# A Mamba-2 scan's chunk loop: `mix` on VectorE, one GpSimd wait fewer, and the w_out split taken two pieces at a time

## What is computed

```python
# token mixing: attention and a bidirectional Mamba-2 scan side by side, one output projection
attn = mla_attention(q_nope, q_rope, k_nope, krope_all, v)          # 4 heads, 128 queries at a time
y = y_f + flip(y_b) + d_skip[:, None] * xs                          # the scan, chunks of 128 tokens
y = y.reshape(b, l, SSM_WIDTH) * silu(z)
ssm_out = rms_norm(y, g_out)                                        # y * rsqrt(mean(y*y)+eps) * g_out
out = concatenate([attn, ssm_out], axis=-1) @ w_out

# inside the scan, for each chunk c of 128 tokens, 8 heads of 64, state 128
lmat  = exp(where(causal, a_cs[..., :, None] - a_cs[..., None, :], -inf))
y_diag = einsum("bgcls,bgrcls,bcsgrp->bclgrp", cb, lmat, xr)        # cb: scores of C against B
state  = state * chunk_decay + chunk_states
y_off  = einsum("bclgn,cbgrpn,bgrcl->bclgrp", cc, entering, exp(a_cs))
```

## Time and profile before

| | |
|---|---|
| median of three runs | 1767.8 us (1766.47 to 1768.09) |
| the profiled execution: time, span | 1768.09 us, 1766.3 us |
| TensorE busy | 1677.5 us, 95% of the span |
| VectorE, ScalarE, GpSimd busy | 1040.2, 725.2, 74.6 us |
| mean granted TensorE clock | 0.982 |
| chunk loop of the scan | about 392 to 480 us |
| attention; its last head | 481 to 801 us; from 738 us |

### The profile page before, as it was taken

One profiled execution on the slowest core, in us unless ns is written; L12 is line 12 of the kernel. 1 busy time (PEld: TensorE's weight loads), 2 busy tenths in 40 slices (PEclk: granted clock), 3 DMA queues, 4 the chain that ended last, 5 costly groups with the idle time before them and its releaser, 6 DMA issues. The chain is left out here.

```text
span 1766.3 us, 24765 instructions
## 1 busy us (share of the span) xinstructions
PE 1677.5 (95%) x9795; PEld 1500.1 (85%) x9795; DVE 1040.2 (59%) x1581; ACT 725.2 (41%) x1208; POOL 74.6 (4%) x116
## 2 busy tenths in 40 slices
PE   6999899999799999999997999999999998999997
PEld 6787788878678888887887999999999997888885
DVE  5855765328755555574568554555545554467777
ACT  5652323334544444463564333333333333434453
POOL 0100000004300000000000000000000000000000
PEclk9999999999999999999999999999999999999998
DMA  9134242002400000114321222222222225573345
GB/s 370 70 131 139 108 147 75 25 33 54 119 14 19 1 13 1 66 37 156 124 96 37 100 86 84 91 88 93 95 82 85 101 76 194 187 234 97 121 145 196
DMA packets 76290, 176.33 MB, mean 100 GB/s; under 512 B 10352, under 2 KB 26944, under 8 KB 74128
## 3 DMA queue, kind: packets, MB, share of 16 engines
q1 hardware_dynamic: 72080, 169.75, 27.7%
q0 software_dynamic: 4096, 5.01, 0.9%
HBM read 131.02 MB, written 43.70 MB: 99 GB/s over the span
## 5 line engine op out<-in xcount | busy, mean ns | idle before, releaser
L409 PE MATMUL psF<-gv,gu_ring 128*128 128x320 f32 x1232 | 382.5, 310 | 9.2 <-issue 4.6
L410 PE MATMUL psF<-gv,gu_ring 128*128 128x320 f32 x1232 | 382.0, 310 | 0.0
L411 PE MATMUL psF<-gv,gu_ring 128*128 128x320 f32 x1232 | 382.0, 310 | 0.0
L409 PEld LDWEIGHTS psF<-gv,gu_ring 128*128 128x128 f32 x1232 | 232.5, 189 | 10.1 <-issue 9.1
L410 PEld LDWEIGHTS psF<-gv,gu_ring 128*128 128x128 f32 x1232 | 232.4, 189 | 0.0
L411 PEld LDWEIGHTS psF<-gv,gu_ring 128*128 128x128 f32 x1232 | 232.3, 189 | 0.0
L409 PE MATMUL psF<-d_w_ring,d_hid_ring 128*128 128x512 f32 x360 | 141.4, 393 | 6.3 <-DVE d_w_ring L2687 6.3
L410 PE MATMUL psF<-d_w_ring,d_hid_ring 128*128 128x512 f32 x360 | 141.6, 393 | 0.0
L411 PE MATMUL psF<-d_w_ring,d_hid_ring 128*128 128x512 f32 x360 | 141.4, 393 | 0.0
L409 PE MATMUL psP<-hT_hi,win_hi 128*128 128x512 f32 (+1 forms) x336 | 122.9, 366 | 2.3 <-DVE hT_lo L184 1.6
L411 PE MATMUL psP<-hT_hi,win_lo 128*128 128x512 f32 (+1 forms) x336 | 119.7, 356 | 0.0
(11 more groups left out here) (425 smaller groups left out, 3622.2 us busy)
## 6 DMA issues: line engine op xcount, KB each, us to landing
hid_variants<-hraw SPq DMA_DIRECT2D x77, 320.0 KB, 2.2
d_hid<-hid_variants SPq DMA_DIRECT2D x77, 320.0 KB, 3.0
m_wring<-in_w_mod SPq DMA_DIRECT2D x16, 1024.0 KB, 5.5
d_b<-in_w_down SPq DMA_DIRECT2D x44, 256.0 KB, 3.8
win_raw<-in_w_in SPq DMA_DIRECT2D x18, 512.0 KB, 5.7
w_mod_staged<-in_w_mod SPq DMA_DIRECT2D x16, 512.0 KB, 11.8
raw_gu<-in_w_gate SPq DMA_DIRECT2D x11, 512.0 KB, 3.9
raw_gu<-in_w_up SPq DMA_DIRECT2D x11, 512.0 KB, 4.8
```

What stands on the lines that cost most here:

```text
L409: pe.matmul(out, w_hi, x_hi, start=first, stop=False, skip_group_check=onto)
L410: pe.matmul(out, w_hi, x_lo, start=False, stop=False, skip_group_check=onto)
L411: return pe.matmul(out, w_lo, x_hi, start=False, stop=last, skip_group_check=onto)
```

## The change

It has four parts.

1. In the scan, the copy of the turned y (`mix`) moves from ScalarE to VectorE, where it is also multiplied with `g_out`. It is done two chunks late, ahead of the off reads; the last two stand after the loop.
2. w_out is accordingly split without the gain, with a plain copy and a plain subtraction.
3. The semaphores `off_f_read` and `off_b_read` become one, `off_read`, raised after both reads. The contribution of chunk 9 moves into the loop, ahead of the diagonal products, and `next_state` is written in line, for every chunk. GpSimd's `decay` no longer waits for `y_ready`.
4. In the last head of attention, the pieces of w_out are split in pairs at t = 2, 4 and 6, on ScalarE after the exponents and on VectorE after the maximum.

```diff
GpSimd, decay(c)
                 pool.wait_ge(sf_ready, c + 1)
-                if c >= 1:
-                    pool.wait_ge(y_ready, c)
                 pool.tensor_tensor(heads(decayed[:]), heads(sf[:, c % 2, :]), across(cdrow[:, c, 0:8], SP_), ALU.mult
...
             # ScalarE: mix(c), its calls mix(c - 1) in the loop and mix(NT - 1) behind it are gone
-            def mix(c):
-                act.wait_ge(y_turned, c + 1)
-                act.activation(zt(c), quads(A[0]), ACT.Copy).then_inc(mix_ready, 1)
...
             # VectorE
+            def mix(c):
+                dve.wait_ge(y_turned, c + 1)
+                dve.tensor_tensor(zt(c), A[0].rearrange("p (a t) -> p a t", a=4),
+                                  across(L.cols[:, C_GS:C_GS + 4], P), ALU.mult).then_inc(mix_ready, 1)
...
             for c in range(NT):
+                if c >= 2:
+                    mix(c - 2)
                 dve.wait_ge(off_done, c + 1)
                 if c >= 2:
                     dve.wait_ge(yn_ready, c - 1)
-                dve.tensor_tensor(heads(yv...), heads(A[1]), ..., ALU.mult).then_inc(off_f_read, 1)
-                dve.tensor_tensor(heads(off_b[:]), heads(A[2]), ..., ALU.mult).then_inc(off_b_read, 1)
-                dve.wait_ge(off_f_read, c + 1)
-                dve.wait_ge(off_b_read, c + 1)
+                f.mark(dve.tensor_tensor(heads(yv...), heads(A[1]), ..., ALU.mult))
+                f.link(dve.tensor_tensor(heads(off_b[:]), heads(A[2]), ..., ALU.mult))
+                dve.sem_inc(off_read, 1)
                 f.link(dve.tensor_tensor(yv[:, c % 2, :], yv[:, c % 2, :], off_b[:], ALU.add))
-                if c + 1 < NT:
-                    next_state(c)
+                (the body of next_state(c))
+                if c + 1 < NT:
                     weights_in_chunk(c + 1)
                 dve.wait_ge(diag_done, c + 1)
...
-            next_state(NT - 1)
+            mix(NT - 2)
             for d in range(2):
                 dve.wait_ge(fin_mm, d + 1)
                 dve.tensor_copy(st_in[:, d, :, :], ...).then_inc(fin_cp, 1)
+            mix(NT - 1)
...
             # TensorE
                 if c >= 1:
-                    pe.wait_ge(off_b_read, c)
+                    pe.wait_ge(off_read, c)
...
                 if c + 1 < NT:
                     segments(c + 1)
-                    pe.wait_ge(off_f_read, c + 1)
-                    contribution(NS + c, c, 0, A[1])
+                pe.wait_ge(off_read, c + 1)
+                contribution(NS + c, c, 0, A[1])
+                if c + 1 < NT:
                     scores(c + 1)
...
-            pe.wait_ge(off_f_read, NT)
-            contribution(NS + NT - 1, NT - 1, 0, A[1])
...
     # OutProj
-        gain = self.L.cols[:, C_GS + k - 4:C_GS + k - 3] if k >= 4 else 1.0
-        act.activation(self.part(k, 0), self.raw(k), ACT.Copy, scale=gain).then_inc(self.hi, 1)
+        act.activation(self.part(k, 0), self.raw(k), ACT.Copy).then_inc(self.hi, 1)
...
     # attention, ScalarE; before: one wo.act_hi(act, t - 2) at each t, ahead of exp at even t and behind it at odd t
+                        if h == HEADS - 1 and t in (2, 4, 6):
+                            act.wait_ge(proj, n_proj(HEADS))
+                            for n in (t - 2, t - 1):
+                                wo.act_hi(act, n)
                         if t >= 4:
                             out(u // 2 - 2)
...
     # attention, VectorE; before: one at each t, at odd t between the pt_lo of groups 0 and 1
+                    if h == HEADS - 1 and t in (2, 4, 6):
+                        for n in (t - 2, t - 1):
+                            wo.dve_lo(dve, n)
                     if t % 2 == 0 and t >= 4:
                         out(u // 2 - 2)
```

More of the change, by code:

```diff
@@ L515, in phase_front @@
         (ones_set, xwf_ready, st_loaded, st_turned, sch, z_done, z_copied, x_turned, x_copied, xw_ready, s_mm,
-         s_ready, cb_done, cb_read, seg_done, exp_done, off_done, off_f_read, off_b_read, w_ready, diag_done, y_ready, squared,
+         s_ready, cb_done, cb_read, seg_done, exp_done, off_done, off_read, w_ready, diag_done, y_ready, squared,
          rstd_ready, yn_ready, y_turned, mix_ready, sf_ready, dec_ready, fin_mm, fin_cp, consts, pch) = (
@@ L520, in phase_front @@
                  "x_copied", "xw_ready", "s_mm", "s_ready", "cb_done", "cb_read", "seg_done", "exp_done", "off_done",
-                 "off_f_read", "off_b_read", "w_ready", "diag_done", "y_ready", "squared", "rstd", "yn_ready", "y_turned", "mix_ready",
+                 "off_read", "w_ready", "diag_done", "y_ready", "squared", "rstd", "yn_ready", "y_turned", "mix_ready",
                  "sf_ready", "dec_ready", "fin_mm", "fin_cp", "consts", "pch"))
@@ L930, in _ @@
                     scale(c - 1)
-                    mix(c - 1)
             square(NT - 1)
             scale(NT - 1)
-            mix(NT - 1)
         @block.vector
@@ L1168, in weights_in_chunk @@
                 dve.tensor_tensor(w, w, cb[:].unsqueeze(2).to_broadcast([P, 2, 4, P]), ALU.mult).then_inc(w_ready, 1)
-            def next_state(c):
+            weights_in_chunk(0)
+            for c in range(NT):
+                if c >= 2:
+                    mix(c - 2)
+                dve.wait_ge(off_done, c + 1)
+                if c >= 2:
+                    dve.wait_ge(yn_ready, c - 1)
+                f.mark(dve.tensor_tensor(heads(yv[:, c % 2, :]), heads(A[1]), across(eoff[:, c, 0:8], SP_), ALU.mult))
+                f.link(dve.tensor_tensor(heads(off_b[:]), heads(A[2]), across(eoff[:, c, 8:16], SP_), ALU.mult))
+                dve.sem_inc(off_read, 1)
+                f.link(dve.tensor_tensor(yv[:, c % 2, :], yv[:, c % 2, :], off_b[:], ALU.add))
                 dve.wait_ge(s_mm, NS + c + 1)
@@ L1521, in act_hi @@
             act.wait_ge(self.extra_loaded, 32)
-        gain = self.L.cols[:, C_GS + k - 4:C_GS + k - 3] if k >= 4 else 1.0
-        act.activation(self.part(k, 0), self.raw(k), ACT.Copy, scale=gain).then_inc(self.hi, 1)
+        act.activation(self.part(k, 0), self.raw(k), ACT.Copy).then_inc(self.hi, 1)
     def dve_lo(self, dve, n):
         k = self.ORDER[n]
-        hi = self.part(k, 0).bitcast(F32)
         dve.wait_ge(self.hi, n + 1)
[L1529 to L1534, removed]
+        dve.tensor_tensor(self.part(k, 1), self.raw(k), self.part(k, 0).bitcast(F32), ALU.subtract).then_inc(self.lo, 1)
     def first_mixes(self):
@@ L1715, in _ @@
                         pt(u - 3, 2)
-                    ahead = h == HEADS - 1 and 2 <= t < 2 + wo.AHEAD
                     if t % 2 == 1:
@@ L1722, in _ @@
                         exp(u - 1)
-                        if ahead:
-                            wo.act_hi(act, t - 2)
                         if t == 1 and h % 2 == 1:
@@ L1727, in _ @@
                     else:
-                        if ahead:
-                            act.wait_ge(proj, n_proj(HEADS))
-                            wo.act_hi(act, t - 2)
                         if t >= 2:
@@ L1850, in _ @@
                         split(h + 1)
-                    ahead = h == HEADS - 1 and 2 <= t < 2 + wo.AHEAD
-                    if ahead and t % 2 == 0:
-                        wo.dve_lo(dve, t - 2)
+                    if h == HEADS - 1 and t in (2, 4, 6):
+                        for n in (t - 2, t - 1):
+                            wo.dve_lo(dve, n)
                     if t % 2 == 0 and t >= 4:
@@ L1856, in _ @@
                     if t >= 2:
[L1857 to L1861, removed]
+                        pt(u - 2, 0, 2)
                     if t >= 1:
```

10 lines of the change are left out of this document (removed).

## The result

The changed kernel took 1775.59 us (median of seven) beside 1767.01 us for the kernel before: a ratio of 1.0054, interval 1.0038 to 1.007. In a second set it took 1777.1 us beside 1764.18 us, a ratio of 1.0093 (1.0077 to 1.0109). A ratio is given here with its 95% interval and is not the quotient of the two medians. It is slower: by 8.6 and 12.9 us in the medians, by 9.5 and 16.4 us if the ratios are taken. 1779.3 was forecast, 11.5 us slower, from 1773 to 1784.

What follows compares the result with a forecast made beforehand. The prediction took TensorE to bound the scan's chunk loop. Its terms, 1.0 + 3.75 + 0 + 0.8 + 4.1 + 1.9 = 11.55 us, on the median of 1767.8 gave 1779.3 us, range 1773 to 1784.

Steps and rivals of the forecast that it cites:

- TensorE bounds the loop, and VectorE's margin is spent: Scan's chunk loop: TensorE sets the 7.95 us period; VectorE's off reads end 0.95 and 0.35 us before the next contribution.
- `decayed` beside the weights: 0.75 us a chunk: Scan's chunk loop: without its wait, `decayed` blocks VectorE's weight lines about 0.9 to 0.95 us; period 8.7 for 7.95.
- By chunk: C(n) is the start of chunk n's contribution on TensorE: C(1) +1.0, C(2) to C(6) +3.75, C(7) +0, C(8) +0.8 us.
- The tail: +4.1: End of the scan: `mix` of chunk 8 comes 4.1 us later, and all of it passes into attention.
- The last head: +1.9: Attention's last head, w_out pieces in pairs: +2.1 us at t=2, -0.1 each at t=4 and t=6.
- The sum: 11.55: Whole kernel: loop, tail and last head together make it 11.55 us slower.
- A: Rival, scan: the blocking by `decayed` stays away; 6.5 us slower, 1774.3 us; chance 0.2.
- B: Rival, last head: value products cover the pairs and the waits on `pt_lo` go, gaining 3.5 us; 1773.9 us; chance 0.1.
- C: Rival, last head: it gains and the scan has no blocking, so the kernel is not slower; 1768.9 us; chance 0.04.
- D: Rival, scan: the change does nothing there, leaving the last head's 1.9 us alone; 1769.7 us; chance 0.04.

Runs made afterwards that it cites:

- before_mix: The kernel before with only `mix` moved to VectorE and the gain taken out of w_out; ratio 1.0005 to the kernel before.
- after_wait: The changed kernel with GpSimd's `decay` waiting for `y_ready` again; ratio 1.005 to the kernel before.
- after_wait_tail: The changed kernel with `decay` waiting for `y_ready` again and the last chunk's contribution back behind the diagonal; ratio 1.0033 to the kernel before.
- before_nowait: The kernel before with only the wait of `decay` on `y_ready` taken away; ratio 1.0018 to the kernel before.
- after: The changed kernel, first set; 1775.59 us, ratio 1.0054 to the kernel before.
- after_head: The changed kernel with the last head's w_out pieces at one per tile again, still without the gain; ratio 1.0048 to the kernel before.
- after_again: The changed kernel repeated without an edit, second set; 1777.1 us, ratio 1.0093 to the kernel before.
- decay_later: The changed kernel with `decay` waiting for `w_ready`, until VectorE's two weight lines are done; ratio 1.0046 to the kernel before.
- before: The kernel before the change, without edits; 1767.01 us in the first set, 1764.18 us in the second.
- pairs_early: The kernel before with the last head's w_out pieces in pairs, on ScalarE ahead of the exponents; ratio 0.9989 to the kernel before.

## Why the prediction was right, step by step

- **TensorE bounds the loop, and VectorE's margin is spent.** Shown: the period is 7.95 us wherever VectorE is not held, also with `mix` on it (`before_mix`), and 8.57 where it is.
- **`decayed` beside the weights: 0.75 us a chunk.** Right in mechanism, a little large: 0.62 us. The block is 0.72 us and not 0.95. The Trainium skill's rule (SBUF — State Buffer, "Who interferes with whom"), that the later of the two waits for the whole instruction of the other, fits both ways round here: `decayed` waits for line 1162, then line 1165 for `decayed`. The 0.72 us is somewhat less than the 0.87 us for which `decayed` is still recorded when line 1165 begins, as the 0.55 us of the earlier trace rows was less than 0.68. Most of the loop's extra time goes with it: 3.8 of 4.4 us come back in `after_wait`.
- **By chunk.** C(1) +1.0 was forecast, with 0.4 us in it that fall ahead of C(0), where the contribution now waits for the second off read. Counted from the first off read of chunk 0, C(0) comes after 1.40 us for 0.99 and C(1) after 9.35 for 8.55: +0.4 and +0.8. C(2) to C(6) were 3.1 for 3.75, C(7) 0.1 for 0, C(8) 0.79 for 0.8: 4.8 for 5.55 together, of which 4.4 lie behind C(0). The block of line 1165 is 0.72 us in chunk 0 too (1.95 for 1.23); its size, taken as 0.9 to 0.95, is what made the loop's terms too large.
- **The tail: +4.1.** It is 4.13 us where the clock holds (25.89 less 21.76) and 6.2 where it falls. Of it the order of the last chunk is 2.35 us (`after_wait_tail`), `mix` behind VectorE's last lines 0.8 (`before_mix`), the longer wait with the blocking 0.7 (25.89 less 25.18). The remaining 0.2 (22.83 in `after_wait_tail` less 22.59 in `before_mix`) is left to the merged semaphore; no run has it alone. The fall of the clock was not foreseen: the forecast has no term for it.
- **The last head: +1.9.** Mis-sized: 3.7 us. At t=2 the step was right (the maximum of the next tile 2.7 us later; by the forecast's two `pt_lo`, 2.8), but the next tile did not give 0.6 us back: it cost another 0.6. TensorE's scores came 8.5 us after the maximum for a forecast of 8.15, and after the wait of 3.18 us the transposes and scores ran slower (1.06 for 0.63 us and 0.77 for 0.48), because the granted clock had fallen to 0.50. TensorE's busy time over the head grew by 1.5 us for the same matmuls, which is most of the 1.8 us that the forecast lacks. So here too the missing term is the clock, which the forecast took as held. What a pair at t=2 would cost at a held clock no trace shows. At t=4 and 6 the pairs cost 0.25 and 0 us, forecast -0.1 each.
- **The sum: 11.55.** With the 0.4 us ahead of C(0) the stages give 14.8 us in the first trace and 12.7 in the second, whose clock held in the tail but not in the head. Of the terms, the loop was 0.75 us too high and the head 1.8 us too low. That the total came out so near has luck in it: these errors have opposite signs, and the medians, 8.6 and 12.9 us, also hold the movement of the two unsteady stretches, as large as any of the errors.
- **The rivals.** A, no blocking, is excluded by lines 712 and 1165. B and C, the last head gains, by the head's 54.4 us; though the odd tiles' waits did go, and with the pairs in another place the head does gain. B's price was misread from the row: of the 3.5 us, 1.25 is the wait behind the last tile, which no placing of the pieces touched, so 2.3 us were there to be won at the value products. D, nothing happens in the scan, by the period; for `mix` alone it would have been nearly right.

## What to carry to other kernels

A wait that looks needless may be what keeps a GpSimd instruction beside VectorE instructions that read PSUM; before removing it, look at what stands on VectorE where the instruction will then land, and how much time the loop's bound has to spare. Count the margins of all edits together: here `mix` alone cost 0.8 us and the free `decayed` alone 1.25, and together with the rest they made the loop VectorE's. And look at the granted clock behind every wait that an edit lengthens: in the last head it made a wait of 3.2 us dearer by some 1.5 us. Work that has to be done early belongs ahead of the operation for which its engine already waits, not behind it.

## What the runs showed of the hardware

- A VectorE instruction that had begun beside one GpSimd instruction did not get its turn before the next one, 0.4 us later: 2.55 us for 1.23 in `before_nowait`. Where VectorE's instruction had begun first, `decayed` took 2.02 us for 1.04 and the next VectorE instruction 1.95 for 1.23.
- The same wait of TensorE, 2.19 us at the same place, was followed by a granted clock of 0.50 in two traces (`after`, 3.51 us for 16 products, and `after_head`) and of 1.00 in a third (`after_again`, 1.90 us). The stage from there to attention took 27.99, 27.50 and 25.89 us: a stall there costs its own length, and in some executions 1.6 or 2.1 us more. A wait of 1.88 us was followed by 0.50 in `decay_later`, one of 1.59 us by 1.00 in `after_wait`.
- Behind the wait of 3.2 us at t=2 of the last head the clock was at 0.50 in all seven traces that have it. With the wait of that tile at 0.46 us (`before`) and 0.65 us (`pairs_early`) it stayed at 1.00.
